# A two-block transformer kernel: step lists in place of expert loops, and the last expert half of three feed-forward stages split by token stream

## The reference, cut to what matters

```python
for e in range(N_EXPERTS):
    out = out + combine[:, e:e + 1].astype(t.dtype) * swiglu(t, wg[e], wu[e], wd[e])
```

```python
def ffn_sublayer(h, shift, scale, gate, w_in, w_out, g, b):
    y = swiglu_2(modulate(h, shift, scale), w_in, w_out)
    return layer_norm_2(ALPHA_2 * h + FFN_RES * gate * y, g, b)
```

## Time and profile before

| | us |
|---|---|
| median of 3 runs | 3549.59 |
| lowest, highest | 3543.07, 3565.11 |
| the profiled execution, its own time | 3536.58 |
| its span (first to last instruction) | 3534.9 |
| PE busy | 3267.3 (92% of the span) |
| DVE, ACT, POOL busy | 1925.4, 1500.8, 571.0 |
| mean granted TensorE clock | 0.945 |

### The profile page before, as it was taken

How to read it: one execution, slowest core, us unless ns; L and a number is a source line. 1 busy time by engine, 2 the same in 40 slices (tenths; PEclk the granted TensorE clock), 3 DMA queues, 4 the chain that set the end, 5 groups by cost and what they waited for, 6 DMA issues and landing times.

```text
span 3534.9 us, 66908 instructions
## 1 busy us (share of the span) xinstructions
PE 3267.3 (92%) x26454; PEld 3081.6 (87%) x26454; DVE 1925.4 (54%) x3108; ACT 1500.8 (42%) x2548; POOL 571.0 (16%) x671
## 2 busy tenths in 40 slices
PE   7779998779999999999999899999998999978898
PEld 7669998569888898999999897699998999965898
DVE  6855559445454454566533753575337633665554
ACT  4335443344444444444422444554224522444444
POOL 3500008400000000022000331151002400230000
PEclk9779999689999999999999999999999999988899
DMA  5314544337777777655432541144324432430253
GB/s 218 127 36 145 185 147 161 87 114 262 266 288 269 276 263 269 224 196 176 144 112 79 184 167 48 48 145 147 118 80 174 168 110 88 136 126 1 103 189 102
DMA packets 101325, 546.27 MB, mean 155 GB/s; under 512 B 16578, under 2 KB 28994, under 8 KB 52331
## 3 DMA queue, kind: packets, MB, share of 16 engines
q1 hardware_dynamic: 84624, 454.93, 36.4%
q0 software_dynamic: 13568, 84.91, 7.1%
q10 hardware_dynamic: 2842, 2.34, 0.2%
HBM read 540.48 MB, written 11.04 MB: 156 GB/s over the span
## 4 chain that ended last, share of the span: by engine, by line
PE 81%; DVE 11%; ACT 4%; issue 2%; POOL 1%; DMA 0%; ACTq 0%; SPq 0%; DVEq 0%; POOLq 0%
PE PS L1016 70%; PE PS L1204 4%; DVE WL L1672 3%; DVE CONV L1900 3%; PE PS L1183 2%; PE PS L1053 2%; PE PS L1193 1%; ACT WH L1334 1%; POOL TMP L923 1%; DVE TMP L2011 1%; PE PS L1158 1%; PE PS L1223 0%; DVE UL L2016 0%; DVE RSTD L1689 0%; ACT PT L1469 0%
## 5 line engine op out<-in xcount | busy, mean ns | idle before, releaser
L1672 DVE TENSOR_TENSOR WL<-RAW,WH 128x1024 fp32r<-128x1024 f32 (+2 forms) x952 | 1077.6, 1135 | 982.4 <-ACT WH L1334 979.6
L1016 PE MATMUL PS<-UH,WH 128*128 128x256 f32 (+1 forms) x5536 | 1458.2, 285 | 124.6 <-DVE H L2024 27.2
L1016 PE MATMUL PS<-UL,WH 128*128 128x256 f32 (+1 forms) x5536 | 1445.4, 283 | 0.0
L1016 PE MATMUL PS<-UH,WL 128*128 128x256 f32 (+1 forms) x5536 | 1444.7, 283 | 0.0
L1334 ACT ACTIVATE WH<-RAW 128x1024 fp32r<-128x1024 f32 (+2 forms) x952 | 913.8, 963 | 1057.6 <-PE PS L1016 1007.3
L1016 PEld LDWEIGHTS PS<-UH,WH 128*128 128x128 f32 x5536 | 1012.2, 193 | 153.6 <-issue 131.1
L1016 PEld LDWEIGHTS PS<-UL,WH 128*128 128x128 f32 x5536 | 1010.1, 192 | 0.3
L1016 PEld LDWEIGHTS PS<-UH,WL 128*128 128x128 f32 x5536 | 1009.6, 192 | 0.0
L1016 PE MATMUL PS<-HIDH,WH 128*128 128x256 f32 (+1 forms) x2112 | 546.9, 279 | 0.0
L1016 PE MATMUL PS<-HIDH,WL 128*128 128x256 f32 (+1 forms) x2112 | 542.6, 277 | 0.0
L1016 PE MATMUL PS<-HIDL,WH 128*128 128x256 f32 (+1 forms) x2112 | 542.4, 277 | 0.0
(11 more groups left out here) (192 smaller groups left out, 2774.4 us busy)
## 6 DMA issues: line engine op xcount, KB each, us to landing
RAW<-in_w_gu SPq DMA_DIRECT2D x222, 1024.0 KB, 4.9
RAW<-in_w_dn SPq DMA_DIRECT2D x168, 704.0 KB, 4.2
MRAW<-in_w_mod POOLq DMA_DIRECT2D x36, 1024.0 KB, 5.2
TMP<-in_w_mod POOLq DMA_DIRECT2D x36, 1024.0 KB, 5.3
RAW<-in_w_in SPq DMA_DIRECT2D x30, 1024.0 KB, 5.3
RAW<-in_w_na SPq DMA_DIRECT2D x20, 1024.0 KB, 4.9
RAW<-in_w_o SPq DMA_DIRECT2D x12, 1024.0 KB, 4.8
RAW<-in_w_proj SPq DMA_DIRECT2D x8, 1024.0 KB, 5.2
```

The source lines that it names most:

```text
L1016: last = pe.matmul(ps[:, a:b], w, m[:, a:b], start=first and a == 0, stop=final and b == n)
L1672: dve.tensor_tensor(WL[slot][:, 0:hi - lo], RAW[:, s % RAW_SLOTS, lo:hi], WH[slot][:, 0:hi - lo].bitcast(F32), ALU.subtract).then_inc(s_lo, 1)
```

## The change

It does three things. The phases `ffn`, `moe` and `fb1` become step lists like `fa0`: one iteration of 38, 152 and 38 steps, written out on SP, PE, ACT and DVE by the same `in_steps`; POOL's loop over the condition's tiles stays. In half 1 of `fa0`, `fb0` and `fa1` all is done for the latent stream (11 ups, 8 downs) and then for the context stream, so the 11 up tiles are loaded and split twice; such a phase has 65 steps. The latent norms behind these phases are hosted by the first 8 context ups. With it come: the order of DVE's last pieces in `ffn` and `fb1` is the usual one, `fb1` puts both results of an up step in one PSUM bank as `moe` did, the full layer norms use banks 1 and 3 in place of 0 and 1, DVE waits for the scaled residual (`s_hs`) only before the first down, and in the last up step of an expert DVE makes its second piece before HIDL.

```diff
-def expert_steps(first, sweeps):
+def expert_steps(first):
...
     steps += [("u", 0, k, BOTH) for k in range(first_ups, KH)]
     steps += [("d", 0, m, BOTH) for m in range(KC)]
-    steps += [("u", 1, k, BOTH) for k in range(KH)]
-    steps += [("d", 1, m, r) for r in (lat_ctx if sweeps else [BOTH]) for m in range(KC)]
+    for r in (LAT, CTXT):
+        steps += [("u", 1, k, r) for k in range(KH)]
+        steps += [("d", 1, m, r) for m in range(KC)]
     return steps
+
+def whole_experts(count, r):
+    return [s for e in range(count) for s in [("u", e, k, r) for k in range(KH)] + [("d", e, m, r) for m in range(KC)]]
...
-            add("ffn", 2, "d" * 19, full + down)
+            add_steps("ffn", "d", whole_experts(2, (0, L1)))
-            add("moe", N_EXP, "d" * 19, full + down)
+            add_steps("moe", "d", whole_experts(N_EXP, LAT))
...
-    add("fb1", 2, "d" * 19, full + down)
+    add_steps("fb1", "d", whole_experts(2, LAT))
...
-    last = {n: ph[n].n - KC for n in ("fa0", "fb0", "fa1")}
+    last = {n: ph[n].n - KH - KC for n in ("fa0", "fb0", "fa1")}
-            HalfNorm(ph, "2a0", 0, "fa0", "fa0", last["fa0"], **long), ...
+            HalfNorm(ph, "2a0", 0, "fa0", "fa0", last["fa0"], **up), ...
...
-        def moe_loop(eng, body):
-            with eng.Fori(0, MOD_EXPERTS) as i:
-                body(i)
-            for i in range(MOD_EXPERTS, N_EXP):
-                body(i)
...
             def begin(p, i, s):
-                if s >= BANK_SETS or p.n_iter > 1:
+                if s >= BANK_SETS:
...
-                        if m < KC - 2 or closing:
-                            ahead(p, i, s, (0,))
-                        elif m == KC - 1:
-                            ahead(p, i, s - 1, (0,))
+                    ahead(p, 0, s, (0,))
```

More of the change, by code:

```diff
@@ L709, in straight, with in_steps @@
                     load(p, 0, s, w[k0 + s])
-            def experts(name, e0):
+            def in_steps(name, e0):
                 p = ph[name]
[L714 to L723, removed]
+                for s, (t, e, k, _) in enumerate(p.steps):
+                    load(p, 0, s, ins["w_gu" if t == "u" else "w_dn"][e0 + e, k])
             def bias_tiles(layer):
@@ L749, in _ @@
                 if i == 0:
-                    experts("ffn", 0)
+                    in_steps("ffn", 0)
                 else:
[L752 to L756, removed]
+                    in_steps("moe", 2)
             for i in range(DEPTH):
@@ L783, in _ @@
                 else:
-                    experts("fb1", 2 + N_EXP + 6)
+                    in_steps("fb1", 2 + N_EXP + 6)
             sp.wait_ge(s_ln, LN_BASE["2b1"] + KC)
@@ L1037, in pair_step @@
                     for j in range(2):
-                        if p.steps or p.name == "moe":
-                            ps, shared = pair_banks(p, s)[j], not p.steps or p.steps[s][3][1] == SEQ
+                        if p.steps:
+                            ps, shared = pair_banks(p, s)[j], p.steps[s][3][1] == SEQ
                         else:
@@ L1078, in chunks @@
                 return lambda k: t[:, k, c0:c0 + n]
[L1080 to L1098, removed]
-                            beside_moe(i, s)
-                        s += 1
-                if name == "moe":
-                    moe_loop(pe, body)
-                else:
-                    iterate(pe, p, body)
             def half_sum(hn, j):
@@ L1157, in norm @@
                     pe.wait_ge(sm, there(c))
-                    last = pe.matmul(PS[0][:, 0:n], ones[:, :], src[:, c, c0:c0 + n], start=(c == 0), stop=(c == cs - 1))
+                    last = pe.matmul(PS[1][:, 0:n], ones[:, :], src[:, c, c0:c0 + n], start=(c == 0), stop=(c == cs - 1))
                 last.then_inc(s_mean, 1)
@@ L1161, in norm @@
                     pe.wait_ge(s_sq, b0 + c + 1)
-                    last = pe.matmul(PS[1][:, 0:n], ones[:, :], TMP[:, c % 4, 0:n], start=(c == 0), stop=(c == cs - 1))
+                    last = pe.matmul(PS[3][:, 0:n], ones[:, :], TMP[:, c % 4, 0:n], start=(c == 0), stop=(c == cs - 1))
                     last.then_inc(s_sqf, 1)
@@ L1283, in _ @@
                     pe.wait_ge(s_silc, 1)
-                experts("moe" if i else "ffn", c0, n)
                 nm = "moe" if i else "ffn"
+                in_steps(nm)
                 if i == 0:
@@ new lines, in half_norm @@
+            def half_norm(hn, j):
+                cols = slice(hn.c0, hn.c0 + SEQ)
+                for c in range(*hn.squares.get(j, (0, 0))):
+                    act.wait_ge(s_ctr, hn.base(c + 1))
+                    if c >= 4:
+                        act.wait_ge(s_s2p, (KC - 1) * hn.q + max(c - 4, 1))
+                    slot, at = hn.square(c)
+                    act.activation(TMP[:, slot, at], H[:, c, cols], ACT.Square).then_inc(s_hsq, 1)
+                if j == hn.rstd:
+                    act.wait_ge(s_hv, hn.q + 1)
+                    act.activation(STD[:, hn.t], PS[7][:, 0:SEQ], ACT.Sqrt, bias=EPST[:, 0:1]).then_inc(s_hstd, 1)
+                for c in range(*hn.make.get(j, (0, 0))[0:2]):
+                    act.wait_ge(s_hva, hn.base(c + 1))
+                    act.activation(UH2[:, c, hn.t], TMP[:, 2 + c % 2, hn.t], ACT.Identity,
+                                   bias=AB[:, hn.table, hn.half, 1, c:c + 1]).then_inc(s_uh, 1)
@@ L1637, in _ @@
             scale_h("fb1", NMETA, SEQ)
-            experts("fb1", SEQ)
+            in_steps("fb1")
             norm("2b1", H, H, V_B + 48 + 32, NMETA, SEQ)
@@ L1734, in beside_moe @@
             def beside_moe(i, s):
-                if not isinstance(i, int):
+                if i < MOD_EXPERTS:
                     return
```

354 lines of the change are left out of this document (134 added, 220 removed).

## The result

The changed kernel takes 3481.99 us (median of four, 3480.01 to 3495.14), the kernel before beside it 3546.33 us (3534.28 to 3565.11). The ratio is 0.9832, 95% interval 0.9801 to 0.9863: 1.7% faster. The forecast was 3497 us, with 3474 to 3529 as the range.

What follows compares the result with a forecast made beforehand. PE's matmuls were taken as the bound, so gains come from its idle and low-clock time. 34.0 + 3.0 + 5.7 + 8.3 - 1.1 + 2.2 = 52.1 us, giving a forecast median of 3497 us, range 3474 to 3529.

Steps and rivals of the forecast that it cites:

- Parts 1 and 2: The moe loop written out saves 34.0 us of idle and slow first steps; small gaps in ffn, moe and fb1 3.0.
- the jump: At each looped moe expert's start, 3.5 us of PE's idle is the hardware loop's branch; rival, a staying wait: 0.09.
- Part 3: Between moe's last expert and fa0, the gap falls from 5.21 to 1.5 us without a slow step: 5.7 us gained.
- Part 4: Ends of fa0, fb0, fa1: 35.0 us of idle and slow steps become 26.7, gaining 8.3; worse-ends rival 0.10.
- I put 0.7 us for it: At each end of fa0, fb0, fa1, the shared RAW slot's late load adds 0.7 us to a 4.3 us gap.
- Part 5: Half 1 of fa0, fb0, fa1: 33 more up steps lie beside PE and cost it 1.1 us in matmul pace.
- The rival of added steps that set the pace: One-stream ups in half 1 not fed in 5.46 us would cost 96 us, 3593 us in all; chance 0.03.
- Part 6: At ffn's end, the usual order of DVE's last pieces lets the norm's subtraction start earlier: 2.2 us gained.
- PE's mean is ready after about 1.4 us: At ffn's end, PE's mean for the norm was taken as ready about 1.4 us on, with DVE's pieces delaying the subtraction.
- Pace: Rival: fewer pauses bring fb1's slower matmul spacing into moe, giving back 28 us, so 3525 us; chance 0.06.

Runs made afterwards that it cites:

- 67 steps: The changed kernel with FIRST_UPS 10 instead of 8, so fa0, fb0 and fa1 have 67 steps each: 3484.52 us in one run.
- the repeat: The changed kernel run once more, nothing altered, in the same set of runs as the lists alone: 3491.68 us, ratio 0.9857 to the kernel before.
- 66: The changed kernel with FIRST_UPS 9 instead of 8, so fa0, fb0 and fa1 have 66 steps each: 3475.71 us, ratio 0.9804.
- 68 in place of 65: The changed kernel with FIRST_UPS 11 instead of 8, so fa0, fb0 and fa1 have 68 steps each: 3466.25 us, ratio 0.9791.
- the kernel with the shortest body: The kernel before, moe loop kept, with an eighth of the condition's products and fewer low-part matmuls in looped experts: 3395.14 us in one run.

## Why the prediction was right, and where a term was off

**Parts 1 and 2: right, cause and size.** The `moe` stage, its first matmul to its last, went from 844.2 us (786.99 to 1636.38 - 5.21) to 807.0. That is 37.2 us; forecast were 34.0 and, for the gaps into experts 6 and 7, 1.6. The step from "looped experts only" to "the jump" was an inference from two kinds of experts in one trace; written out with the stores kept, the gaps went. The Trainium skill, Runtime: NRT & Kernel Launch, Instruction fetch mechanics, makes a taken branch cost a fetch where its target lies outside the window of pages that the engine holds. PE's runs bear this out, gaps and packets both, but the limit lies between 1655 and 1728 recorded instructions, not at the 2048 that the page gives as PE's store. ACT paused with some 310 recorded instructions in an iteration (looped expert 1), fewer than the 512 that the page gives for such an engine; with some 140 in an iteration of `ffn` it did not. No run varied ACT's body, so for ACT this is one observation and no measured limit.

**Part 3: right.** 5.21 + 7.46 became 1.61 + 5.72: 5.3 us of the 5.7.

**Part 4: mechanism right, one term too small.** I gave 26.7 us to stay: 4.2 for POOL, 15.0 of gaps, 7.5 of slow steps. It was 4.1, 17.6 and 8.1 (8.44 + 8.19 + 7.89 - 3 x 5.46), 29.8 in all. So 5.2 us were gained and not 8.3. The term that failed is "I put 0.7 us for it", the shared RAW slot: 67 steps against 65 make it 1.4. The chain at the end of `fb0` shows it:

```profile
2669.17 0.75 ACT WH L1296
2669.95 1.33 DVE WL L1605
2671.29 5.19 DMA RAW<-in_w_gu
2676.51 1.06 ACT WH L1296
2677.59 1.22 DVE WL L1605
2678.82 0.40 DVE H L1714
2679.21 2.80 DVE WL L1605 x2
2682.01 0.41 DVE H L1714
```

Step 64's low part frees the RAW slot at 2671.28, the load takes 5.19 us, and ACT has its tile only when PE is at its end. I had let ACT begin 1.7 us before it, right behind PE's first piece, and made the load 0.7 late on that. The rest of the sequence is, term by term, the sum of the prediction: 1.06 + 1.22 + 0.40 + 2.80 + 0.41.

**Part 5: right in kind.** The 66 pieces are there, half 1 is fed without a wait (2280 matmuls in 258.44 us, 113.35 ns each). The rival of added steps that set the pace is refuted.

**Part 6: the order right, the size not, and nothing left of it at `moe`.** The step that failed is "PE's mean is ready after about 1.4 us". Before and after, in PE's timeline:

```profile
492.21 3.83 PE L1158 MATMUL PS<-H,ONES 128*128 128x272 f32 x16
490.66 3.83 PE L1120 MATMUL PS<-H,ONES 128*128 128x272 f32 x16
```

The mean's matmuls take 3.83 us, so before it was ready at 496.04, only 0.9 us ahead of the subtraction at 496.92. Now the subtraction follows it at once, at 494.60. Counted from the mean's start, 4.71 us became 3.94: 0.8 us gained, forecast 2.2. The rest of the 2.3 us between 496.92 and 494.60 is, to 0.2 us, part 2 and a program that was 1.1 us ahead before `ffn` began (its first matmul at 292.51 instead of 293.65). At the start of `moe` nothing is left: from `ffn`'s first matmul it is 493.34 us before and 493.63 in the changed kernel (493.86 in the repeat), for the profile has a new wait of 1.54 us for WL at 604.67, behind DVE's convolution. That stage is bound by DVE there, and I should have looked at what follows before I booked the gain, that of `ffn` in part 2 included.

**Pace: the rival came true in other runs, not in this one.** The differences measured make 0.9 (at the start of `moe`, where by part 6 it is not the change's) + 37.2 + 5.3 + 5.2 + 0.8 (`fb1`) = 49.4 us, and the profile shows 41.4. All of the difference falls behind the start of `fa0`, and lies in the spacing of matmuls, as far as I can count it. I took PE's matmul starts in blocks of sixteen, and for each block without a pause whose mean spacing is 115.5 to 119.5 ns counted what is over 113.4: 10.7 us before, 19.1 in the changed kernel's profile. These 8.4 us close the account to 0.4, though a fit so good is partly luck: the count sees nothing in the attention stages, where pauses stand in every block, and of the 12.1 us between the spans of the two profiles of this kernel it explains 3.6.

Nothing ties it to the change: the count gives 5 to 25 us in the five profiles of kernels without the full lists, and 9 to 26 in the eight with them. The repeat of the same kernel has 15.5 us of it. Its longest stretch, in `fb0`, stands in the same place as in the first profile, the one in `fa1` is gone, and `fa0` has a new one; so the question put to the repeat, code or execution, has no clean answer. My rival had fewer pauses bring this pace into `moe`. That stage took 807.0 us in both profiles of the changed kernel, at 113.4 ns. But with 66 and with 67 steps, where its code is the same, it took 812.9 us, with some 160 us at 117.9 ns: 6 us of the 28 that the rival allowed for.

**The number.** The forecast for the median, 3497, was 15 us high. The sum was 52.1; the traces give the change 48.2 (37.2 + 5.3 + 5.2 + 0.8 - 0.3). The profiled executions differ by 41.4, less than the sum, and the medians by 64.3, more than it. So the largest term was right in cause and size, but how close the median came is also the luck of which executions were profiled and in which set the kernel was timed: its median is 3482 in one set and 3492 in another. The range held both.

## What to carry to other kernels

Look at the trace behind each jump of a hardware loop, for each engine: idle time with no releaser there is the jump's own price. In this kernel it was 0 or 3.5 us on TensorE, by the size of its body, and a pause of over 4 us cost another 2.5 us at the lower clock. The profile page's count of instruction packets tells whether a body is fetched again. Where a list of steps cycles through slots, write down its length modulo each slot count, the load buffers' too, before choosing how steps are split; here 68 in place of 65 was worth 21 us by the traces (14.0 of idle and 6.8 of slow steps), and the split at 65 was worth 5.2. And check when the inputs of the second stream's first step are made: one step too early cost 11 us. Before booking a gain at the end of one stage, look at what bounds the next: `ffn`'s gains were gone at `moe`.

## What the runs showed of the hardware that I had not expected

**Two spacings at one clock.** At a granted clock of 1.00, long runs of 256-column matmuls go at 113.4 or at 117.9 ns, and at nothing between. In the changed kernel's profile (the chain above) 1992 matmuls from 2354.90 take 234.87 us, 117.9 ns each, and the 582 from 2603.16 take 65.99, 113.4 each. The window says the same of the clock, and its DMA share, 0.44, is no higher than the 0.47 of the window over `fa0` above, which ran at the quick spacing. First the profile of the changed kernel, then its repeat, where the stretch stands again:

```profile
2354.90:2589.77 234.87, 234.87 (x1993) 234.87 (x1994) 115.46 (x148) 87.54 (x122) 6.35 (x8) 1.00 0.44 151
2354.90:2589.77 234.87, 234.87 (x1995) 234.84 (x1995) 115.41 (x148) 87.58 (x123) 6.24 (x8) 1.00 0.44 151
```

Between two interruptions of PE (a pause, or a norm's matmuls) the spacing does not change: leaving out the kernel with the shortest body, every such run of over 150 matmuls of 256 columns keeps one of the two from first to last, in all thirteen profiles, the longest over 2791 matmuls. The same run can have either: that of 1990 matmuls in `fa1` from 2738 goes at 117.9 ns in the first profile and at 113.4 in the repeat. Counted as above, the slower spacing costs between 5 and 26 us in these profiles, as much as the smaller effects that the study set out to measure. What decides it when PE starts again I don't know, and no run here was made to find out.

**A jump that is paid twice.** PE and ACT pause independently at the same jump (4.74 us before PE's first matmul of expert 1, 3.55 before ACT's table load 4 us later). Only PE's reached the end of the kernel. Straight code, which fetches all of its instructions once, showed no such price: the some 7500 matmuls of the written-out `moe` stage follow each other without a pause of 0.5 us.
